# A decoder step on one core: six projection units contraction-outermost in six PSUM banks, modulation weights by 512 columns in buffers of their own

## The chip, the core and the metric

The kernel runs on one core of a Trainium2 chip. The metric is the device time of one execution in microseconds. TensorE (PE) multiplies and transposes into PSUM (8 banks of 512 float32 per partition), ScalarE (ACT), VectorE (DVE) and GpSimd (POOL) do the elementwise work, SyncE's queue (SP) issues nearly all loads from HBM, strictly in the order written. Each engine runs its own program; they meet in semaphores.

## What is computed

One layer for 256 prompt tokens and 8 x 4 sample tokens (288 columns, TOK). Cut to what matters:

```python
mod = (silu(c) @ w_ada + b_ada).reshape(B, 6, 1, D)     # w_ada: 1024 x 6144
sh1, sc1, g1, sh2, sc2, g2 = [mod[:, i] for i in range(6)]
h = x * (1 + sc1) + sh1
qa, ka, va, qb, kb, vb, ga, gb = split(h @ w_in)        # w_in: 1024 x 5120
# rotary on q and k; dilated attention (A) and block attention (B), with caches
merged = sigmoid(ga) * (oa @ w_pa) + sigmoid(gb) * (ob @ w_pb)
x = layer_norm(ALPHA * x + g1 * (merged @ w_o))
h2 = x * (1 + sc2) + sh2
up, gt = split(h2 @ w_up);  f = (silu(gt) * up) @ w_down
x = layer_norm(ALPHA * x + g2 * f)
```

The new keys and values, and shifted caches, are outputs too.

## The kernel before

Activations lie transposed: 8 blocks (KT) of 128 channels by 288 tokens. A projection is done in **units** of 128 output columns (`unit_mm`, L668): for each of 8 contraction blocks three matmuls of 288 columns (`mm3`, L662: high x high, high x low, low x high of a float32 split in two), 24 in one PSUM bank, then an eviction. A unit therefore can't start before its bank is free nor finish before all of h is there. The weights of one unit are a **half**: ScalarE copies it to `w_hi` (L473), VectorE writes the remainder to `w_lo` (L478). There are four places for halves (SPLIT), and ACT and DVE split half nb + 4 right behind the eviction of unit nb.

All weights arrive through one ring, `raw`, of three slots of 1 MB (RAW). `free_slot` (L523) makes SP wait until the piece three before has been used: a piece of w_in, w_up and so on once both halves are split (`lo_ready`), a modulation chunk once its matmuls are done (`ada_used`).

**Modulation** (`ada_mm`, L681): silu(c), 9 rows padded to 32, is the stationary operand; a chunk of 256 columns of w_ada needs eight matmuls, four at a time in the four 32-column strips of the array. ScalarE copies the result to `rowbuf` (`ada_rows`, L1119), TensorE turns it and sums the strips (`ada_turn`, L693, two matmuls), VectorE adds the bias (`ada_add`, L1371). There are 24 chunks: 8 before the projection (shift and scale of h), 12 one by one between the unit pairs, 2 at the output projection and 2 at the second modulation.

**The projection** runs over c = 0 to 11, two units each, in banks 0 and 1; six of the c are queries or keys of which ACT makes a first copy (L1150), DVE a shuffled one (L1428) and POOL and DVE the rotation (the list ROPED); c = 6, 7, 8 and 11 are values. Then eight steps j transpose values and keys to rows (L768), then `keys_turn` (L784) transposes the cached keys of the samples, with scores, gate units and so on behind.

**SP's order** in the projection: w_in pieces and modulation chunks in turn; the masks; from the ninth piece on the cached keys of sample 0 to 3 (`load_kv`, L556, five DMAs each) between them; then the first two pieces of gate weights (GATE0, GATE0 + 1, L606) behind the last piece of the projection; only then a wait for the transposes. The first two gate halves are split in the last pair but one's order, as nb + 4 says.

Of the kernel before, what the change touches and what calls it, by code (L numbers as in the profile page):

```python
# [7 lines left out]
F32 = mybir.dt.float32  # L8
# [177 lines left out]
MIX_N = 12  # L186
# [91 lines left out]
def build(nc, x_prompt, x_sample, cache_a, cache_rows, cache_b, page_table, c_prompt, c_sample, w_ada, b_ada, w_in,  # L278
# [24 lines left out]
    kvin, _ = sb("kvin", [128, 2, 6, 256])  # L303
# [7 lines left out]
    rowbuf, _ = sb("rowbuf", [128, 3, 256])  # L311
# [3 lines left out]
    rows, _ = sb("rows", [64, 128])  # L315
# [42 lines left out]
    st6, _ = sb("st6", [128, 3, 4, 6])  # L358
# [19 lines left out]
    c_zero, c_ready, ada_used, first_in = sem("c_zero"), sem("c_ready"), sem("ada_used"), sem("first_in")  # L378
# [53 lines left out]

    def raw_half(n_static_slot, hh, by_rows):

        if by_rows:
            return raw[:, n_static_slot, 1024 * hh:1024 * hh + 1024]
        return raw8(n_static_slot)[:, :, 128 * hh:128 * hh + 128]
# [22 lines left out]
    def part(t, slot, by_rows):  # L460
        if by_rows:
            return t[:, slot, :]
        return t[:, slot, :].rearrange("p (k n) -> p k n", k=8)

    def split_hi(act, nb, slot4, rslot, hh, need, by_rows=False):

        if isinstance(nb, int) and nb == 0:
            act.wait_ge(first_in, 16)
        else:
            act.wait_ge(raw_in[rslot], need)  # L470
# [32 lines left out]

    PAB_BANK = (0, 1, 6, 3)
# [14 lines left out]
    def _(sp):  # L519
# [3 lines left out]
        def free_slot(n):  # L523

            m = n - RAW
            if m >= 0 and ada_chunk(m) is not None:
                sp.wait_ge(ada_used, N_ADA_BEFORE[m] + 1)
# [6 lines left out]

        def load_ada(n):
            a = ada_chunk(n)
            load(n, n % RAW, w_ada_v[:, :, 256 * a:256 * a + 256], raw8(n % RAW))

        for n in range(MIX0):
            load_ada(n)  # L540
            if n == 0:
                sp.dma_start(rows[0:48, :], b_ada.rearrange("a (j p) -> (a j) p", p=128)).then_inc(rows_in, 16)
                sp.dma_start(rows[48:56, :], ln1_g.rearrange("a (j p) -> (a j) p", p=128)).then_inc(rows_in, 16)
                sp.dma_start(rows[56:64, :], ln1_b.rearrange("a (j p) -> (a j) p", p=128)).then_inc(rows_in, 16)
            if n == 2:
                sp.dma_start(x_tok[:, 0:2, :], x_prompt.rearrange("a (t p) d -> p (a t) d", p=128)).then_inc(x_in, 16)
                sp.dma_start(x_tok[0:SAMPLE, 2, :], x_sample.rearrange("b t d -> (b t) d")).then_inc(x_in, 16)
# [38 lines left out]

        for n in range(MIX0, GATE0):
            c = (n - MIX0) // 2
            if n == MIX0:
                free_slot(n)  # L590
                sp.dma_start(raw8(n % RAW)[:, :, 0:128], w_in_v[:, :, 0:128]).then_inc(first_in, 16)
                sp.dma_start(raw8(n % RAW)[:, :, 128:256], w_in_v[:, :, 128:256]).then_inc(raw_in[n % RAW], 16)
                sp.dma_start(cst[:, C_COS:C_MS], const[:, C_COS:C_MS]).then_inc(tables_in, 16)
                sp.dma_start(pages[:], page_table.rearrange("b n -> (b n)").unsqueeze(0)).then_inc(pages_in, 16)
            elif ada_chunk(n) is None:
                load(n, n % RAW, w_in_v[:, :, 256 * c:256 * c + 256], raw8(n % RAW))
            else:
                load_ada(n)
            if n == MIX0 + 9:
                sp.dma_start(cst[:, C_MS:C_END], const[:, C_MS:C_END]).then_inc(masks_in, 16)  # L600
                sp.wait_ge(pages_in, 16)
            if MIX0 + 9 <= n < MIX0 + 9 + DEC_B:
                look_up_pages(n - MIX0 - 9)
            if n > MIX0 + 9 and n % 2 and (n - MIX0 - 11) // 2 < 4:
                load_kv((n - MIX0 - 11) // 2, 0)
# [72 lines left out]
    def ada_bank(i):  # L678
        return {20: 5, 21: 4, 22: 7, 23: 2}.get(i, 5 + i % 3)

    def ada_mm(pe, n):  # L681

        i, slot, bank = N_ADA_BEFORE[n], n % RAW, ada_bank(N_ADA_BEFORE[n])
        pe.wait_ge(raw_in[slot], raw_need(n, slot))
        if i >= 3:
            pe.wait_ge(ada_mod, i - 2)
        for k in range(KT):
            q = 32 * (k % 4)
            mm = nc.tensor.matmul(psum[q:q + 32, bank, 0:256], c_z[:, k, :], raw8(slot)[:, k, :], start=(k < 4), stop=(k >= 4),  # L689
                                  skip_group_check=True)  # L690
        mm.then_inc(ada_used, 1)

    def ada_turn(pe, i):  # L693

        pe.wait_ge(ada_row, i + 1)
        for hh in range(2):
            mm = nc.tensor.matmul(psum[:, ada_bank(i), 256 + 9 * hh:256 + 9 * hh + 9], rowbuf[:, i % 3, 128 * hh:128 * hh + 128],  # L697
                                  cst[:, C_ADA:C_ADA + 9], start=True, stop=True, skip_group_check=True)
        mm.then_inc(ada_turned, 1)

# [5 lines left out]
    def _(pe):  # L706
# [22 lines left out]
        for i in range(N_ADA0):  # L729
# [1191 lines left out]
```

## Time and profile before

| | us |
|---|---|
| median of 3 runs | 564.42 |
| lowest, highest | 560.51, 568.14 |
| the profiled execution | 561.89 |
| its span | 560.3 |
| PE busy | 516.1 (92%) |
| DVE busy | 290.5 (52%) |
| ACT busy | 223.5 (40%) |
| POOL busy | 92.2 (16%) |

PE's busy time is modelled, since matmuls are pipelined: PE at 92% waits little, but may be at half pace. Where the first matmuls run, the distance between their starts tells the pace. Times of rows are microseconds from the start of the span.

### The profile page before, as it was taken

How to read it: one execution, taken by the hardware profiler on the slowest of the kernel's cores; microseconds unless marked ns; L12 is line 12 of the kernel's file. 1: busy time of each engine (PE TensorE's matmuls, PEld its weight loads, DVE VectorE, ACT ScalarE, POOL GpSimd, SP SyncE). 2: the span in 40 equal slices, each digit the busy share in tenths (PEclk: the TensorE clock that was granted, in tenths of full speed). 3: DMA queues.
4: the chain of work that ended last, by engine and by line, in shares of the span. 5: the costliest groups of instructions: out<-in, count | busy, mean ns of one | idle time of the engine just before them, and what ended most of it. 6: DMA issues, size and time to landing. Idle time of an engine off the chain costs nothing.

```text
span 560.3 us, 10315 instructions
## 1 busy us (share of the span) xinstructions
PE 516.1 (92%) x4051; PEld 473.0 (84%) x4051; DVE 290.5 (52%) x561; ACT 223.5 (40%) x377; POOL 92.2 (16%) x127
## 2 busy tenths in 40 slices
PE   4787999999999989999989979999999999999990
PEld 2546899989978979897789869999999999999980
DVE  0055657556743453353587595546555544435356
ACT  1042424333344454253643645465444344333311
POOL 1000123002770000000055053601111100000005
PEclk9999899999999999998999979999999999999995
DMA  8987699998185982194433474898876745354002
GB/s 280 340 267 231 208 359 348 338 303 293 38 285 173 303 279 77 42 274 142 151 116 114 148 225 132 302 329 289 264 278 216 272 159 182 120 187 171 17 1 84
DMA packets 96719, 116.78 MB, mean 208 GB/s; under 512 B 3596, under 2 KB 87756, under 8 KB 96165
## 3 DMA queue, kind: packets, MB, share of 16 engines
q1 hardware_dynamic: 94788, 102.76, 56.3%
q0 software_dynamic: 1888, 13.44, 6.6%
q8 instruction: 30, 0.49, 0.4%
q14 instruction: 13, 0.10, 0.1%
HBM read 112.90 MB, written 13.57 MB: 226 GB/s over the span
## 4 chain that ended last, share of the span: by engine, by line
PE 77%; DMA 9%; DVE 4%; ACT 3%; SPq 2%; issue 2%; POOL 2%; POOLq 0%; DVEq 0%; ACTq 0%
PE psum L664 21%; PE psum L666 20%; PE psum L665 20%; DMA raw<-in_w_in 6%; PE psum L689 3%; PE psum L784 3%; DMA raw<-in_w_ada 2%; PE psum L900 2%; PE psum L697 2%; PE psum L844 1%; PE psum L886 1%; DVE w_lo L478 1%; PE psum L853 1%; PE psum L798 1%; ACT qkvg L1206 1%
## 5 line engine op out<-in xcount | busy, mean ns | idle before, releaser
L478 DVE TENSOR_TENSOR w_lo<-raw,w_hi 128x1024 fp32r<-128x1024 f32 x118 | 146.7, 1244 | 169.6 <-ACT w_hi L473 169.4
L664 PE MATMUL psum<-act_hi,w_hi 128*128 128x288 f32 x736 | 223.9, 304 | 9.2 <-DVE act_lo L1647 3.5
L665 PE MATMUL psum<-act_lo,w_hi 128*128 128x288 f32 x736 | 219.6, 298 | 0.0
L666 PE MATMUL psum<-act_hi,w_lo 128*128 128x288 f32 x736 | 219.0, 298 | 0.0
L473 ACT ACTIVATE w_hi<-raw 128x1024 fp32r<-128x1024 f32 x118 | 124.1, 1056 | 138.3 <-PE psum L666 90.7
L664 PEld LDWEIGHTS psum<-act_hi,w_hi 128*128 128x128 f32 x736 | 140.5, 191 | 17.9 <-issue 11.0
L666 PEld LDWEIGHTS psum<-act_hi,w_lo 128*128 128x128 f32 x736 | 141.0, 192 | 0.0
L665 PEld LDWEIGHTS psum<-act_lo,w_hi 128*128 128x128 f32 x736 | 140.8, 191 | 0.1
L664 PE MATMUL psum<-f_hi,w_hi 128*128 128x288 f32 x176 | 52.4, 298 | 0.6 <-DVE f_t L1685 0.6
L665 PE MATMUL psum<-f_lo,w_hi 128*128 128x288 f32 x176 | 51.9, 295 | 0.0
L666 PE MATMUL psum<-f_hi,w_lo 128*128 128x288 f32 x176 | 51.8, 294 | 0.0
L1789 POOL TENSOR_TENSOR qkvg<-qkvg,cst 128x288 f32 (+1 forms) x16 | 16.6, 1036 | 121.0 <-ACT qkvg L1150 121.0
L689 PE MATMUL psum<-raw,c_z 128*32 128x256 f32 x384 | 32.4, 468 | 4.4 <-DMA raw<-in_w_ada 4.3
L664 PEld LDWEIGHTS psum<-f_hi,w_hi 128*128 128x128 f32 x176 | 33.0, 187 | 0.9 <-issue 0.8
L666 PEld LDWEIGHTS psum<-f_hi,w_lo 128*128 128x128 f32 x176 | 33.1, 188 | 0.0
L665 PEld LDWEIGHTS psum<-f_lo,w_hi 128*128 128x128 f32 x176 | 33.0, 188 | 0.0
L1823 POOL TENSOR_TENSOR qkvg<-qkvg,gated 128x288 f32<-128x288 f32 x8 | 8.4, 1079 | 120.0 <-DVE gated L1597 120.0
L697 PEld LDWEIGHTS psum<-cst,rowbuf 128*128 128x128 f32 x96 | 16.0, 235 | 11.9 <-ACT rowbuf L1121 6.2
L1874 POOL DMA_DIRECT2D out<-in_cache_kv_a x24 | 11.7, 488 | 77.4 <-PE psum L666 75.8
L689 PEld LDWEIGHTS psum<-raw,c_z 128*32 128x32 f32 x384 | 11.5, 125 | 13.3 <-DMA raw<-in_w_ada 5.4
L1314 ACT ACTIVATE silu_t<-psum 128x288 f32<-128x288 f32 x22 | 9.0, 409 | 33.5 <-PE psum L666 33.5
L697 PE MATMUL psum<-cst,rowbuf 128*128 128x9 f32 x96 | 16.7, 284 | 5.0 <-ACT rowbuf L1121 5.0
(190 smaller groups left out, 556.4 us busy)
## 6 DMA issues: line engine op xcount, KB each, us to landing
raw<-in_w_ada SPq DMA_DIRECT2D x24, 1024.0 KB, 7.1
raw<-in_w_up SPq DMA_DIRECT2D x22, 1024.0 KB, 7.0
raw<-in_w_in SPq DMA_DIRECT2D x19, 1024.0 KB, 7.0
raw<-in_w_down SPq DMA_DIRECT2D x10, 1024.0 KB, 5.0
out<-in_cache_kv_a POOLq DMA_DIRECT2D x16, 504.0 KB, 6.1
raw<-in_w_o SPq DMA_DIRECT2D x4, 1024.0 KB, 4.8
kvin<-in_cache_kv_a SPq DMA_DIRECT2D x8, 256.0 KB, 3.1
kvin<-in_cache_kv_b SPq DMA_DIRECT2D x16, 128.0 KB, 3.4
```

What stands on the lines that cost most here:

```text
L473: nc.scalar.activation(part(w_hi, slot4, by_rows), raw_half(rslot, hh, by_rows), ACT.Copy).then_inc(hi_ready, 1)
L478: nc.vector.tensor_tensor(part(w_lo, slot4, by_rows), raw_half(rslot, hh, by_rows), part(w_hi, slot4, by_rows).bitcast(F32), ALU.subtract) ...
L664: nc.tensor.matmul(out, hi_l, hi_r, start=start, stop=False, skip_group_check=True)
L665: nc.tensor.matmul(out, hi_l, lo_r, start=False, stop=False, skip_group_check=True)
L666: return nc.tensor.matmul(out, lo_l, hi_r, start=False, stop=stop, skip_group_check=True)
L689: mm = nc.tensor.matmul(psum[q:q + 32, bank, 0:256], c_z[:, k, :], raw8(slot)[:, k, :], start=(k < 4), stop=(k >= 4), skip_group_check=True)
L697: mm = nc.tensor.matmul(psum[:, ada_bank(i), 256 + 9 * hh:256 + 9 * hh + 9], rowbuf[:, i % 3, 128 * hh:128 * hh + 128], cst[:, C_ADA:C_ADA ...
L784: mm = nc.tensor.transpose(psum[:, bank, col:col + nr], kv_tiles(b, 0, tile)[0:nr, 0, 128 * hp:128 * hp + 128], cst[0:nr, 0:nr])
L900: mm = nc.tensor.matmul(psum[:, 6, E * i:E * i + E], prbT[:, u % 2, 128 * n:128 * n + 128], tok[:, kb, 1, 256 * g + E * h:256 * g + E * h ...
L1314: nc.scalar.activation(silu_t[:, q, :], psum[:, q, 0:TOK], ACT.Silu).then_inc(silu_ready, 1)
L1789: nc.gpsimd.tensor_tensor(block_at(qkvg, blk), block_at(qkvg, blk), cst[:, C_COS:C_COS + TOK], ALU.mult).then_inc(cos_done, 1)
L1874: pool.dma_start(kv_sample[g][bass.ds(b, 1), 0:BUF[g] - DEC_T, :], cache_rows[g][bass.ds(b, 1), DEC_T:BUF[g], :]).then_inc(moved, 16)
```

## The change

- Modulation weights are read by 512 columns and half of the contraction: a **part** q is 4 contraction blocks x 512 columns, 1 MB as before, four matmuls of 512 columns. Two parts (2i, 2i + 1) add up in a bank; one row copy of 512, one turn of four matmuls and one add follow for both. Parts 0 to 19 go to five buffers `ada_s`, which lie in space that is unused so early: two in `qkvg`'s value and query blocks, one in its gate blocks, where later keys of sample 2 lie, one in `kvin`, one in `tmp`, where later keys of sample 3 lie. Parts 20 to 23 still use the ring.
- Of w_in, blocks 12 to 17 (the values, c = 6 to 8) come first, as four ring pieces of 2 contraction blocks x 768 columns. Their six units run contraction-outermost in banks 0 to 5: step k does all six units' three matmuls of block k. So step 0 needs only h's first block. Splits are of 768 columns, one for each k.
- The other nine c (MIX_C) follow as before, with 12 parts spread over the nine rounds m (MIX_ADA: 2, 1, 1, 2, 1, 1, 2, 1, 1), and six turns, each between a round's two units.
- SP loads in the order shown. Keys of samples 0 and 1 are issued behind part 19; those of sample 2 wait for 19 parts used and those of sample 3 for 20; the gate weights stand behind them.
- Units are counted anew (H_MIX 8, H_GATE 26, was 0 and 24), so slots of halves and of the ring shift.

```diff
+MIX_C = (0, 1, 2, 3, 4, 5, 9, 10, 11)
+FIRST_BLK, FIRST_N = 12, 6
+ADA_ORDER = (0, 2, 1, 3, 4, 5, 6, 7, 8, 9, 10, 11)
+ADA_BANK = (6, 7, 6, 7, 6, 7, 6, 7, 6, 7, 5, 7)
+ADA_BUF = (0, 1, 2, 3, 4, 0, 1, 2, 3, 4, 2, 3, 4, 2, 3, 4, 2, 4, 2, 4)
+MIX_ADA = [range(N_ADA0 + (4 * m + 2) // 3, N_ADA0 + (4 * m + 6) // 3) for m in range(9)]
...
+        def load_start(q):
+            last = [p for p in range(q) if ADA_BUF[p] == ADA_BUF[q]]
+            if last:
+                sp.wait_ge(ada_used, last[-1] + 1)
+            sp.dma_start(ada_s[ADA_BUF[q]][:], ada_part(q)).then_inc(start_in[ADA_BUF[q]], 16)
...
+        load_start(2)
+        load_start(3)
+        load_start(4)
+        load_start(5)
+        load_first(0)
+        load_first(1)
+        load_start(6)
+        load_start(7)
+        load_first(2)
+        load_first(3)
...
+        load_start(8)
+        load_start(9)
+        load_mix(0)
+        load_start(10)
+        load_mix(1)
+        load_mix(2)
+        load_mix(3)
+        load_start(11)
...
+        load_mix(7)
+        load_start(17)
+        load_start(18)
+        load_mix(8)
+        load_start(19)
+        load_kv(0, 0)
+        load_kv(1, 0)
+        sp.wait_ge(ada_used, 19)
+        load_kv(2, 0)
+        sp.wait_ge(ada_used, 20)
+        load_kv(3, 0)
         load_static(GATE0)
         load_static(GATE0 + 1)
...
+    def first_mm(pe, k):
+
+        pe.wait_ge(lo_ready, k + 1)
+        pe.wait_ge(h_lo, k + 1)
+        for q in range(FIRST_N):
+            c = 128 * q
+            mm = mm3(psum[:, q, 0:TOK], w_hi[:, k % SPLIT, c:c + 128], w_lo[:, k % SPLIT, c:c + 128], act_hi[:, k, :], act_lo[:, k, :],
+                     k == 0, k == KT - 1)
...
+        ada_start(pe, 0)
+        ada_start(pe, 1)
+        ada_turn(pe, 0)
+        pe.wait_ge(rows_ready, 1)
+        turn_x()
+        ada_start(pe, 2)
+        ada_start(pe, 3)
+        ada_turn(pe, 1)
+        ada_start(pe, 4)
+        ada_start(pe, 5)
+        first_mm(pe, 0)
+        ada_turn(pe, 2)
+        first_mm(pe, 1)
+        ada_start(pe, 6)
+        ada_start(pe, 7)
+        first_mm(pe, 2)
+        ada_turn(pe, 3)
+        for k in range(3, KT):
+            first_mm(pe, k)
+
+        for m in range(9):
+            for q in MIX_ADA[m]:
+                ada_start(pe, q)
             for hh in range(2):
...
+                nb = H_MIX + 2 * m + hh
+                pe.wait_ge(acc_free[hh], m + 1)
+                unit_mm(pe, nb, nb % SPLIT, hh)
+                if hh == 0 and m in ROWS_AT:
+                    ada_turn(pe, ROWS_AT[m])
```

On ACT the last two rounds of the projection and the first eviction of the transposing steps. Before (L1150 evicts a unit, L473 splits a half, L1121 copies rows, raw_in2 is the ring slot of the first gate weights):

```order
L1121 ACTIVATE rowbuf<-psum 128x256 [waits ada_used]
L1150 ACTIVATE qkvg<-psum 128x288 [waits half_used]
L473 ACTIVATE w_hi<-raw 128x1024 [waits half_used,raw_in2]
L1150 ACTIVATE qkvg<-psum 128x288 [waits half_used]
L473 ACTIVATE w_hi<-raw 128x1024 [waits half_used,raw_in2]
L1121 ACTIVATE rowbuf<-psum 128x256 [waits ada_used]
L1159 ACTIVATE tok<-psum 128x2x128 [waits tok_turned]
```

Of the change, the same place (L1245, L484 and L1203 are the same three operations; raw_in1 is the slot of the first gate weights; the last L1203 copies the rows of parts 18 and 19):

```order
L1245 ACTIVATE qkvg<-psum 128x288 [waits half_used]
L484 ACTIVATE w_hi<-raw 128x1024 [waits half_used,raw_in1]
L1245 ACTIVATE qkvg<-psum 128x288 [waits half_used]
L484 ACTIVATE w_hi<-raw 128x1024 [waits half_used,raw_in1]
L1203 ACTIVATE rowbuf<-psum 128x512 [waits ada_used]
L1252 ACTIVATE tok<-psum 128x2x128 [waits tok_turned]
```

In both the two splits of the gate weights stand around the second eviction of the last round but one and ahead of the last row copy; what differs is when the weights are issued. On SP, before (L533 a ring piece, L559 the first of the five DMAs of a sample's keys), the last six pieces of the projection and the two of the gate:

```order
L565 DMA k_late<-in_cache_kv_b 128x256
L533 DMA raw<-in_w_in 128x8x256 [waits ada_used]
L533 DMA raw<-in_w_ada 128x8x256 [waits lo_ready]
...
L533 DMA raw<-in_w_in 128x8x256 [waits ada_used]
L533 DMA raw<-in_w_in 128x8x256 [waits lo_ready]
L559 DMA k_extra<-in_cache_kv_a 128x256 [waits tok_turned]
```

Of the change (L545 a ring piece, L594 to L600 keys), behind the last modulation part:

```order
L594 DMA k_early<-in_cache_kv_a 128x256 [waits ada_used]
...
L594 DMA k_late<-in_cache_kv_a 128x256 [waits ada_used]
L595 DMA k_late<-in_cache_kv_a 128x2x256
L597 DMA k_late<-in_cache_kv_a 64x1x256
...
L600 DMA k_late<-in_cache_kv_b 128x256
L545 DMA raw<-in_w_in 128x8x256 [waits lo_ready] x2
L594 DMA k_extra<-in_cache_kv_a 128x256 [waits tok_turned]
```

The keys of sample 3 (k_late), which stood before the last modulation chunks, now stand behind the last one's use, with the gate weights (x2) behind them.

## Rows read from the trace of the kernel before

**Rows 1.** Chain of waits, 0 to 200 us: start, length, what.
```profile
10.30 10.03 DMA raw<-in_w_ada
...
50.81 5.22 DMA raw<-in_w_in
...
131.53 0.34 PE psum L697 x4
131.87 1.00 PE psum L689 x16
...
139.45 0.35 PE psum L697 x4
...
153.17 5.42 PE psum L784 x36
```

**Rows 2.** Stretches: length; busy of PE, PEld, DVE, ACT, POOL; granted clock, DMA share, GB/s.
```profile
4.00:28.00 24.00, 16.48 (x113) 10.42 (x116) 1.27 (x7) 1.78 (x5) 0.00 (x0) 1.00 1.08 349
28.00:32.00 4.00, 4.00 (x36) 1.92 (x28) 0.18 (x1) 1.36 (x3) 0.00 (x0) 1.00 0.32 89
58.00:60.00 2.00, 2.00 (x22) 1.42 (x22) 1.97 (x5) 1.01 (x2) 1.03 (x1) 0.83 0.09 28
60.00:147.00 87.00, 86.30 (x724) 80.01 (x723) 52.06 (x112) 28.35 (x44) 18.25 (x37) 0.98 0.88 291
```

**Rows 3.** Timeline of PE, 43 to 64 us: start, length, line, idle before.
```profile
44.03 0.61 PE L664 MATMUL psum<-act_hi,w_hi 128*128 128x288 f32 x1 [3.17 <-DVE w_lo L478]
...
48.76 0.44 PE L665 MATMUL psum<-act_lo,w_hi 128*128 128x288 f32 x1
49.00 0.35 PE L666 MATMUL psum<-act_hi,w_lo 128*128 128x288 f32 x1
49.18 0.30 PE L664 MATMUL psum<-act_hi,w_hi 128*128 128x288 f32 x1
...
57.43 0.61 PE L697 MATMUL psum<-cst,rowbuf 128*128 128x9 f32 x4 [3.29 <-ACT rowbuf L1121]
...
62.70 0.33 PE L665 MATMUL psum<-act_lo,w_hi 128*128 128x288 f32 x1
```

**Rows 4.** Timeline of PE, 8 to 24 us, modulation chunks and a turn.
```profile
12.76 1.03 PE L697 MATMUL psum<-cst,rowbuf 128*128 128x9 f32 x4
...
20.37 1.94 PE L689 MATMUL psum<-raw,c_z 128*32 128x256 f32 x16 [3.61 <-DMA raw<-in_w_ada]
```

**Rows 5.** Timeline of DVE and ACT, 28 to 48 us and 142 to 145.
```profile
29.97 1.08 ACT L1132 ACTIVATE xT<-psum 128x512 f32<-128x512 f32 x2
...
35.23 0.23 DVE L1383 TENSOR_TENSOR qkvg<-xT,mod 128x64 f32<-128x64 f32 x1
...
35.75 0.74 DVE L1387 TENSOR_SCALAR qkvg<-xT,mod 128x256 f32<-128x256 f32 x2
...
39.17 2.29 DVE L1392 TENSOR_TENSOR act_lo<-qkvg,act_hi 128x288 fp32r<-128x288 f32 x6
...
46.17 2.36 DVE L478 TENSOR_TENSOR w_lo<-raw,w_hi 128x1024 fp32r<-128x1024 f32 x2 [0.32 <-ACT w_hi L473]
...
143.29 0.81 DVE L1443 COPY qz<-qkvg 64x32 f32<-64x32 f32 x4
```

**Rows 6.** Timeline of ACT and of SP's queue: a late split, key and gate loads.
```profile
56.05 1.06 ACT L473 ACTIVATE w_hi<-raw 128x1024 fp32r<-128x1024 f32 x1 [5.85 <-DMA raw<-in_w_in]
...
105.41 0.58 SPq L559 DMA_DIRECT2D k_late<-in_cache_kv_a  x1
...
108.56 0.50 SPq L533 DMA_DIRECT2D raw<-in_w_in  x1
...
132.93 2.09 SPq L533 DMA_DIRECT2D raw<-in_w_in  x2
...
151.55 0.34 SPq L559 DMA_DIRECT2D k_extra<-in_cache_kv_a  x1
...
153.15 0.98 SPq L565 DMA_DIRECT2D k_extra<-in_cache_kv_b  x2
```

More of the change, by code:

```diff
@@ L431, in raw8, with raw4 @@
         return raw[:, slot, :].rearrange("p (k n) -> p k n", k=8)
+    def raw4(slot):
+        return raw[:, slot, :].rearrange("p (k n) -> p k n", k=4)
     def raw_half(n_static_slot, hh, by_rows):
+        if by_rows == "first":
+            return raw[:, n_static_slot, FIRST_COLS * hh:FIRST_COLS * hh + FIRST_COLS]
         if by_rows:
@@ L460, in part @@
     def part(t, slot, by_rows):
+        if by_rows == "first":
+            return t[:, slot, 0:FIRST_COLS]
         if by_rows:
@@ L465, in split_hi @@
     def split_hi(act, nb, slot4, rslot, hh, need, by_rows=False):
[L467 to L470, printed above, removed]
+        act.wait_ge(raw_in[rslot], need)
         if not isinstance(nb, int) or nb >= SPLIT:
@@ L484, in halves @@
         for n in range(first, last):
-            by_rows = PAB0 <= n < WO0 or n >= DOWN0
+            by_rows = "first" if n < MIX0 else PAB0 <= n < WO0 or n >= DOWN0
             for hh in range(n_halves(n)):
@@ L502, in lo_static @@
             split_lo(dve, nb, s, r, hh, by)
+    ROWS_AT = {m: q // 2 for m, qs in enumerate(MIX_ADA) for q in qs if q % 2}
     PAB_BANK = (0, 1, 6, 3)
@@ L533, in load, with ada_part @@
             sp.dma_start(dst, src).then_inc(raw_in[slot], 16)
+        def ada_part(q):
+            j, a = ADA_ORDER[q // 2], q % 2
+            return w_ada_v[:, 4 * a:4 * a + 4, 512 * j:512 * j + 512]
         def load_ada(n):
[L536 to L547, printed above, removed]
+            load(n, n % RAW, ada_part(ada_chunk(n)), raw4(n % RAW))
@@ L585, in load_static, with load_mix @@
                 load(n, n % RAW, w_up_v[:, :, col:col + 256], raw8(n % RAW))
[L587 to L605, printed above, removed]
+        def load_mix(m):
+            n, c = MIX0 + m, MIX_C[m]
+            load(n, n % RAW, w_in_v[:, :, 256 * c:256 * c + 256], raw8(n % RAW))
+        load_start(8)
[6 more added lines that the diff above has]
+        load_start(11)
+        sp.dma_start(cst[:, C_MS:C_END], const[:, C_MS:C_END]).then_inc(masks_in, 16)
+        sp.wait_ge(pages_in, 16)
+        look_up_pages(0)
+        look_up_pages(1)
+        load_mix(4)
+        load_start(12)
+        look_up_pages(2)
+        look_up_pages(3)
+        load_mix(5)
+        load_start(13)
+        load_start(14)
+        look_up_pages(4)
+        look_up_pages(5)
+        load_mix(6)
+        load_start(15)
+        load_start(16)
+        look_up_pages(6)
+        look_up_pages(7)
+        load_mix(7)
[9 more added lines that the diff above has]
+        load_kv(3, 0)
         load_static(GATE0)
@@ new lines, in _ @@
+        for j in range(2):
+            dve.wait_ge(turned_x, j + 3)
+            V.tensor_copy(xT[:, 4 * j:4 * j + 4, 128:256],
+                          psum[:, 3 + j, :].rearrange("p (k c) -> p k c", c=128)).then_inc(x_ready_dve, 1)
+        dve.wait_ge(turned_x, 5)
+        V.tensor_copy(xT[:, :, PROMPT:TOK], psum[:, 0, 0:256].rearrange("p (k c) -> p k c", c=SAMPLE)).then_inc(x_ready_dve, 1)
+        dve.wait_ge(x_ready_act, 2)
+        dve.wait_ge(x_ready_dve, 3)
+        ada_add(1)
+        modulate_pair(0)
@@ L1420, in _ @@
+        lo_static(dve, 5)
         rest_of(qkvg, 6, h_hi, h_lo)
         rest_of(qkvg, 7, h_hi, h_lo)
-        for nb in range(H_MIX + 1, H_MIX + AHEAD):
+        for nb in range(6, 11):
             lo_static(dve, nb)
+        for q in (1, 3, 5):
+            if q < 5:
+                dve.wait_ge(first_done, q + 1)
+            else:
+                dve.wait_ge(half_used, KT)
+            V.tensor_copy(qkvg[:, FIRST_BLK + q, :], psum[:, q, 0:TOK]).then_inc(acc_free[1] if q == 1 else v_free, 1)
@@ L1578, in _ @@
         oT_rest(1)
-        ada_add(20)
         def merged_rest(m):
```

269 lines of the change are left out of this document (137 added, 132 removed).

## Prediction, made before the changed kernel ran

> **What bounds the kernel now.** I read the chain of waits of the first 200 us, the stretches beside it, and then TensorE's own instructions. The chain [rows 1] shows two stages. Up to 59 us it hangs on loads and on what follows them: 10.03 us for a piece of w_ada, 5.22 us for a piece of w_in issued at 50.81. From there it is TensorE almost alone: between the turns at 131.53 and 139.45 lie 7.92 us, which are 0.34 for the turn, 1.00 for one modulation chunk and 6.58 for two projection units, 24 matmuls each. In 60 to 147 TensorE is busy 86.3 of 87 us [rows 2]. The units end one such round behind 139.45, at 147.4, eight transposing steps follow, and key turning (L784) begins at 153.17. What the change can win must come from before 59 us, where six units' work can be put under the loads; after that only the sum of TensorE's work counts, and any new wait adds to it.
>
> The loads of the start are not at their limit throughout: 349 GB/s in 4 to 28, but 89 in 28 to 32 and 28 in 58 to 60, because the three-slot ring waits for its readers [rows 2]. At 349 GB/s a piece of 1.05 MB takes 3.0 us.
>
> **TensorE's pace.** The first unit starts at 44.03, one matmul of 288 columns each 0.24 us, which is 1.2 GHz; from 49.18 on it is the pace of 6.58 us for 48 matmuls, 0.137 each with its gaps, 2.4 GHz. The ring then starves it 3.29 us (to 57.43), and up to 62.70 the pace is 0.24 again [rows 3]; the granted clock, 1.00 in most rows, is 0.83 in 58 to 60 [rows 2], so I go by the starts of matmuls. The modulation matmuls before 40 us all ran at the slow pace: 1.94 us a chunk, 1.03 a turn of two matmuls [rows 4].
>
> **Step 1: the start.** First load, second load, x, and the next two modulation parts carry the same bytes as the three chunks, x and the fourth chunk did, so the fourth part lands at 20.4, as the fourth chunk did [rows 4]. Behind it, in issue order at 3.0 us for 1.05 MB and 2.3 for the 0.79 MB pieces of w_in: parts 5 and 6 at 23.4 and 26.4, w_in 0 and 1 at 28.7 and 30.9, parts 7 and 8 at 33.9 and 36.9, w_in 2 and 3 at 39.2 and 41.5. Buffers of their own let them follow without a gap. TensorE: parts 3 and 4 end about 23.7, their turn (now four matmuls, 2.0 us slow, after a row copy of 1.08/2 = 0.54) at 26.4, parts 5 and 6 at 30.3. VectorE's two modulations take twice 0.23, then 0.74 for two blocks, and gaps, 1.3 us a pair; splitting 768 columns takes three quarters of 1.18 on VectorE, 0.9, and as much on ScalarE; a rest (act_lo) is 2.29/6 = 0.4 [rows 5]. The first of the eight steps of the six-bank stage then starts at about 31, when w_in 0 is split: 18 matmuls, 4.3 us slow or 2.4 fast. In order: step 0 to 35.3; turn to 37.3; step 1, mostly fast, to 40; parts 7 and 8 (2.0) to 42; step 2 to 44.4; turn (0.7) to 45.1; step 3 to 47.5. Step 4 needs the second half of h: add, two modulation pairs, a split and a rest, 0.2 + 2.6 + 0.9 + 0.4 behind the turn, so 49.2, a wait of 1.7. Four more steps: **58.9**. By then the old kernel had done two units and ten chunks; this one has done six units and eight.
>
> **Step 2: the remaining 18 units.** Nine rounds of 6.58 [rows 1], twelve parts of 1.00, six turns of twice 0.34: 59.2 + 12.0 + 4.1 = 75.3, so they would end at 134.2 against 147.4, a gain of **13.2**. A part of 4 matmuls on 512 columns streams as many columns as 8 on 256. No row has that form; nearest is the chunk, 1.00 fast and 1.94 slow. I take 1.00; without its gaps 0.8 is possible (12 x 0.2 = 2.4 less), and if 512 columns in four strips overlap worse, 1.94 is the far end (11 more). VectorE and ScalarE keep the work per round that they had and have slack: of 87 us VectorE is busy 52 and ScalarE 28 [rows 2].
>
> **Step 3: the wait that the change brings.** Here the listing of the order decides. SP's queue is strictly in order. The fourth set of keys (k_late) now lies where part 19's buffer was, and is issued only after all 20 parts are used; the first gate weights stand behind it. Part 19 is used at the head of the last round. But these gate halves are split two rounds ahead in ScalarE's and VectorE's order, in the last round but one, in front of the eviction of its second unit and of the last row copy. In the old kernel the gate weights were issued at 132.93, 14.5 us before the units ended [rows 6]. Now: part 19 used at T. The five key loads hold SP 3.1 us (105.41 to 108.56 [rows 6]). The gate load lands 5.2 us after issue with nothing ahead (50.81 to ScalarE's start at 56.05 [rows 1, 6]). Then ScalarE: split 1.06, eviction 0.4, split 1.06, row copy 0.55: T + 11.4. TensorE has in that time only one unit, 3.3; it then waits in the turn of the last rows for **8.1 us**. Behind that turn stand the last unit and all transposes, and VectorE, waiting for the same halves, is no earlier. Bounds: the key loads took 2.6 at least (151.55 to 154.13 [rows 6]), and a load in a full queue 8 (a chunk of 3.0 ahead of it): the wait lies between 7.6 and 11. The clock pays too: after 3.29 us idle the pace was slow for 3.6 us, at the first unit for 5 [rows 3]. So the turn costs 2.0 instead of 0.7, and the last unit has 15 to 20 matmuls at 0.24 instead of 0.134, 1.6 to 2.1: **3.1** together, 0 if the clock held.
>
> **Step 4: the tail.** The four query copies (0.81 [rows 5]) now fall in the last round, ahead of the first key copy: **0.7** later. From there on every wait hangs on what TensorE has done and moves with it; the last two modulation chunks have half the row copies, under half a microsecond, which I leave out. The ring's slots are numbered anew but hold as many pieces.
>
> **Sum.** 13.2 - 8.1 - 3.1 - 0.7 = 1.3 us earlier at L784. The profiled execution takes 561.9 (span 560.3, and what lies around it stays), so 560.6. It lies 2.5 below the median of 564.4; on the median's scale the sum is 563.1. I forecast **561.5**, between the two. (2%, about what a measurement of this kernel can tell, is 11.3 us.)
>
> **Rivals.**
> The gate wait is hidden: slower key turning or the sequence of semaphores lets the last unit run first. For it: all the weights but these are long there. Against: T + 11.4 has no cover but one unit, and even the shortest key loads leave 7.6. It gives 561.9 - (13.2 - 0.7) = 549.4. A cheaper cousin, parts at 0.8, no slow clock and the shortest wait, gives 560.6 - 2.4 - 3.1 - 0.5 = 554.6.
>
> The slower side: the contraction-outermost stage never gets the fast clock. Its steps are 2.4 us bursts between waits and modulation matmuls, and the modulation matmuls alone ran at the slow pace for 20 us though TensorE was busy [rows 4]. Seven more steps at 0.24 cost 18 x 0.106 x 7 = 13.4, less the 1.7 of the wait, plus 2.6 for two parts and a turn: 14.3 more, 574.9 on the profile's scale, 577 on the median's. Each slow step costs 1.9, so one undoes the 1.3 of the sum, and with seven the change is slower by 2%. Against: the longest pause in my order is 1.7, and 1.35 us of turn and chunk between units never slowed it in 60 to 147.
> The Trainium skill, TensorE: Matmul & The Clock Gate, section HAM oscillation, speaks for this rival: a kernel that walks the contraction and waits for a load between its steps falls back to 1.2 GHz each time, and it advises finishing the contraction of one output before waiting. By that rule the time would be the rival's 574.9; the trace's pause of 3.29 us agrees with the rule, but no row has so short a pause as the ones here.
>
> A second late load: the weights of the last round are issued behind part 18, whose buffer frees only in round 6 (109.8), and land about 118 (a second load lands 3 after the first). ScalarE then evicts round 6's second unit late, and its bank is free about 120.8, 1.4 us before TensorE wants it. If loads are 2 or 3 us slower, TensorE waits 1 to 2 more there and the key loads move along: 562 to 565.
>
> **Numbers.** Forecast as summed 0.67 (its own range 556 to 567); gate wait hidden or mostly paid back 0.13; slow clock in the six-bank stage 0.06; second late load 0.10; something else in the ring 0.04. The range 551 to 568 leaves out part of the hidden wait and the slow clock. Faster by over 2% (below 553.1) 0.14, slower 0.06, between 0.80.
>
> **What would show it.** Right: the first matmul of six banks near 31, the stage over near 59 with a 1 to 2 us gap before step 4; rounds of 7.6 or 8.3 or 9.3; a DMA of w_in issued near 130 in the chain, TensorE idle about 8 us before the last turn, slow pace behind it; L784's first turn near 151 to 152. Wrong: no idle stretch near 130, a six-bank stage over after 65 with steps of 4.3, or parts that take other than 1.0.

## The result, and the profile after

| | before | after |
|---|---|---|
| median of 20 runs each | 563.17 | 566.10 |
| lowest, highest | 559.09, 568.14 | 563.32, 569.53 |
| ratio after to before, with its 95% interval | | 1.006 (1.0036 to 1.0084) |
| span of the profiled execution | 560.3 | 564.4 |
| PE busy | 516.1 | 510.9 |
| DVE, ACT, POOL busy | 290.5, 223.5, 92.2 | 294.4, 222.9, 89.1 |

The change makes the kernel 0.6% slower, where about 0.5% faster was forecast (561.5 against the 564.42 known then). TensorE is busy 5.2 us less and the span is 4.1 us longer, so about 9 us of waits have come in. The line numbers of after that matter: L721 to L723 are `mm3`, L742 the matmuls of a part, L756 the turn, L484 and L489 the splits on ScalarE and VectorE, L1203 the row copy, L1549 the query copies, L852 and L853 the transposes of values and keys, L868 key turning, L1911 GpSimd's scaling of x, L545 a ring load.

The chain of waits of after, 120 to 156 us (start, length, what), from the last modulation part to key turning:

```profile
122.83 1.04 PE psum L742 x8
123.89 0.34 SPq L594
...
126.49 5.88 DMA raw<-in_w_in
...
133.74 0.94 ACT w_hi L484
134.69 0.50 ACT rowbuf L1203
135.22 1.88 PE psum L756 x8
...
142.47 0.46 DVE qkvg L1561
143.03 4.66 DVE qz L1549
...
149.05 0.66 PE psum L852 x2
...
154.17 1.95 PE psum L868 x13
```

Before, these 30 us were nearly all TensorE ([rows 1]: a turn, a chunk, units). Now they hold two stalls: the gate load that was forecast, and behind it 4.66 us in one query copy of VectorE, which was not. Key turning starts at 154.17, 1.0 later than in [rows 1].

The stretches of after (columns as in [rows 2]):

```profile
4.00:28.00 24.00, 16.30 (x97) 8.03 (x97) 4.92 (x14) 4.29 (x9) 0.00 (x0) 0.86 1.03 388
28.00:32.00 4.00, 3.32 (x15) 3.35 (x16) 3.61 (x10) 2.79 (x6) 0.00 (x0) 0.61 1.05 410
...
130.00:140.00 10.00, 4.78 (x21) 4.78 (x22) 4.49 (x8) 2.79 (x4) 3.87 (x17) 0.57 0.48 158
140.00:155.00 15.00, 10.16 (x68) 9.00 (x68) 10.54 (x22) 4.25 (x16) 7.49 (x11) 0.83 0.08 24
```

The start answers to [rows 2]: 388 GB/s where 349 were moved, 410 where 89 were. From 130 to 155 TensorE is busy 14.9 of 25 us, at a granted clock of 0.57 and 0.83.

The timeline of TensorE in after, the six-bank stage and the start of the nine rounds behind it (idle before in brackets):

```profile
23.87 1.92 PE L742 MATMUL psum<-ada_s,c_z 128*32 128x512 f32 x16
28.68 0.39 PE L721 MATMUL psum<-act_hi,w_hi 128*128 128x288 f32 x1 [2.88 <-DVE act_lo L1483]
...
32.67 0.95 PE L756 MATMUL psum<-cst,rowbuf 128*128 128x9 f32 x8
...
45.41 0.37 PE L721 MATMUL psum<-act_hi,w_hi 128*128 128x288 f32 x1 [1.58 <-DVE act_lo L1483]
55.12 1.92 PE L742 MATMUL psum<-ada_s,c_z 128*32 128x512 f32 x16
```

The stage starts at 28.68 and is over at 55.12, 3.8 us before the forecast.

### The profile page after: what moved, and what is told of

Read it like the earlier page. It is cut to its first block, busy times and chain, and to the rows that moved or that the text cites. A ratio compares the mean times of both kernels' runs of the same rounds, so it can differ in the third digit from the quotient of the medians.

```text
span 564.4 us, 9903 instructions
## 1 busy us (share of the span) xinstructions
PE 510.9 (91%) x3859; PEld 464.0 (82%) x3859; DVE 294.4 (52%) x548; ACT 222.9 (39%) x370; POOL 89.1 (16%) x127
## 4 chain that ended last, share of the span: by engine, by line
PE 81%; DMA 6%; DVE 6%; issue 2%; ACT 2%; SPq 2%; POOL 1%; POOLq 0%; DVEq 0%; ACTq 0%
PE psum L721 22%; PE psum L723 21%; PE psum L722 21%; DMA raw<-in_w_in 5%; PE psum L742 3%; PE psum L868 3%; PE psum L984 2%; PE psum L756 1%; PE psum L928 1%; DMA ada_s<-in_w_ada 1%; PE psum L970 1%; PE psum L937 1%; PE psum L882 1%; DVE qz L1549 1%; ACT w_hi L484 1%
## 5 line engine op out<-in xcount | busy, mean ns | idle before, releaser
L721 PE MATMUL psum<-act_hi,w_hi 128*128 128x288 f32 x736 | 224.6, 305 | 8.9 <-DVE act_lo L1483 4.5
L489 DVE TENSOR_TENSOR w_lo<-raw,w_hi 128x1024 fp32r<-128x1024 f32 (+1 forms) x120 | 147.1, 1228 | 163.0 <-ACT w_hi L484 162.8
L723 PE MATMUL psum<-act_hi,w_lo 128*128 128x288 f32 x736 | 219.5, 298 | 0.0
L484 ACT ACTIVATE w_hi<-raw 128x1024 fp32r<-128x1024 f32 (+1 forms) x120 | 124.6, 1041 | 128.0 <-PE psum L723 96.1
L721 PEld LDWEIGHTS psum<-act_hi,w_hi 128*128 128x128 f32 x736 | 141.0, 192 | 22.1 <-issue 13.9
L723 PEld LDWEIGHTS psum<-act_hi,w_lo 128*128 128x128 f32 x736 | 141.2, 192 | 0.0
L721 PE MATMUL psum<-f_hi,w_hi 128*128 128x288 f32 x176 | 52.4, 298 | 0.6 <-DVE f_t L1787 0.6
L723 PE MATMUL psum<-f_hi,w_lo 128*128 128x288 f32 x176 | 51.8, 294 | 0.0
L721 PEld LDWEIGHTS psum<-f_hi,w_hi 128*128 128x128 f32 x176 | 33.0, 187 | 0.9 <-issue 0.8
L723 PEld LDWEIGHTS psum<-f_hi,w_lo 128*128 128x128 f32 x176 | 33.2, 188 | 0.0
L1891 POOL TENSOR_TENSOR qkvg<-qkvg,cst 128x288 f32 (+1 forms) x16 | 14.5, 906 | 117.4 <-ACT qkvg L1245 117.4
L756 PEld LDWEIGHTS psum<-cst,rowbuf 128*128 128x128 f32 x96 | 12.6, 203 | 14.4 <-ACT rowbuf L1203 14.4
L742 PE MATMUL psum<-ada_s,c_z 128*32 128x512 f32 x160 | 23.1, 683 | 0.6 <-DMA ada_s<-in_w_ada 0.6
L756 PE MATMUL psum<-cst,rowbuf 128*128 128x9 f32 x96 | 12.7, 260 | 10.2 <-ACT rowbuf L1203 10.2
L1245 ACT ACTIVATE qkvg<-psum 128x288 f32<-128x288 f32 x16 | 6.5, 408 | 36.1 <-PE psum L723 36.1
```

The costliest lines, as they stand in the source:

```text
L484: nc.scalar.activation(part(w_hi, slot4, by_rows), raw_half(rslot, hh, by_rows), ACT.Copy).then_inc(hi_ready, 1)
L489: nc.vector.tensor_tensor(part(w_lo, slot4, by_rows), raw_half(rslot, hh, by_rows), part(w_hi, slot4, by_rows).bitcast(F32), ALU.subtract) ...
L721: nc.tensor.matmul(out, hi_l, hi_r, start=start, stop=False, skip_group_check=True)
L723: return nc.tensor.matmul(out, lo_l, hi_r, start=False, stop=stop, skip_group_check=True)
L742: mm = nc.tensor.matmul(psum[32 * kk:32 * kk + 32, ADA_BANK[i], :], c_z[:, 4 * a + kk, :], src[:, kk, :], start=(a == 0), stop=(a == 1), s ...
L756: mm = nc.tensor.matmul(psum[:, ADA_BANK[i], 9 * hh:9 * hh + 9], rowbuf[:, i % 2, 128 * hh:128 * hh + 128], cst[:, C_ADA:C_ADA + 9], start ...
```

## The experiments

Nine kernels ran; all times are in us. The first four shared one chip and its runs of the kernel before (median 563.63), the next four another (562.86), the last one a third series (562.19). Where two of my kernels are compared, it is by the spans and rows of their profiles, and by the ratio to before where that is said.

**Queries a round earlier.** Why did a copy of 64 x 32 elements take 4.7 us? The order on VectorE puts the query copies behind the last unit's eviction; GpSimd, which waits only for the last rotation, is by then in its long scaling of x (6.04). This kernel makes the copies one round (m) earlier.

```diff
-            if m == 8:
+            if m == 7:
                 queries_by_row(3)
```

> The changed kernel, with the last four query copies one round earlier on VectorE (m = 7, their inputs are long there). In the changed kernel they take 5.31 us together, where the kernel before had 0.81, beside a 6.04 us operation of GpSimd (the scaling of x). Theory A: they are held by GpSimd's operation running at the same time; moved to where GpSimd is between its rotation and its key copies they take about 1 us, key turning starts 4 to 5 us earlier than 154.17 (149 to 150), the time falls by 4 to 5 us to about 561.5 and the wait of 8.0 us before the last turn stays. Theory B: the copies are slow because of what they read (a wait or a bank of their inputs), then they stay near 5 us wherever they stand and the time stays at 566.

Measured: median 556.3 (555.25 to 559.65), ratio 0.988 (0.982 to 0.995), span 554.0. The copies and GpSimd's scaling in this run (two rows of the timelines of DVE and POOL):

```profile
138.69 0.81 DVE L1549 COPY qz<-qkvg 64x32 f32<-64x32 f32 x4
...
142.81 6.04 POOL L1911 TENSOR_SCALAR xT<-xT 128x2304 f32<-128x2304 f32 x1
```

and in after:

```profile
141.62 6.04 POOL L1911 TENSOR_SCALAR xT<-xT 128x2304 f32<-128x2304 f32 x1
...
142.95 5.31 DVE L1549 COPY qz<-qkvg 64x32 f32<-64x32 f32 x4
```

Ahead of the scaling four copies take 0.81; begun 1.3 us into it they take 5.31, and the first alone ends at 147.71, 0.05 behind the scaling's end at 147.66. Key turning starts at 148.62, 5.5 earlier than in after, while the wait for the gate weights stays (8.96). So the two stalls are separate. The gain in the span, 10.4 (9.8 by the medians), is more than the 5.5 at key turning and more than the 4 to 5 expected: further on, TensorE's pause ahead of the prompt's transposes shrinks from 3.54 to 1.81 and no slow matmuls follow it (3.2 together), and the second group of matmuls on the sample values takes 3.00 instead of 4.61 (4.52 before, so that part is not an effect of the copies alone).

**Gate weights first.** This takes the forecast wait away by issuing the two loads ahead of the keys that wait for parts 18 and 19.

```diff
         load_kv(1, 0)
+        load_static(GATE0)
+        load_static(GATE0 + 1)
         sp.wait_ge(ada_used, 19)
         load_kv(2, 0)
         sp.wait_ge(ada_used, 20)
         load_kv(3, 0)
-        load_static(GATE0)
-        load_static(GATE0 + 1)
```

> The changed kernel, with the first two pieces of gate weights issued on SP ahead of the keys of samples 2 and 3, so that they wait for nothing that the last round does. Theory A: TensorE's wait of 8.0 us ahead of the last turn goes, and with it the slow pace of the turn and of the last unit (1.1 and 2.0 us): 11 us less up to the end of the units (about 131 instead of 142.3). GpSimd's scaling of x follows the last rotation, so it begins near 131 and still meets the query copies: those stay near 5 us. Time about 555. Rival: another load takes the place (the key loads of sample 3 or the weights of the last round), the wait only shrinks to 3 to 5 us and the time is 560 to 563.

Measured: median 555.02 (549.56 to 559.1), ratio 0.987 (0.979 to 0.994), span 548.0. TensorE ahead of the last turn, and the chain's gate load:

```profile
128.96 1.06 PE L756 MATMUL psum<-cst,rowbuf 128*128 128x9 f32 x8 [1.29 <-ACT rowbuf L1203]
```

```profile
117.02 9.08 DMA raw<-in_w_in
```

The wait falls from 8.02 to 1.29, the slow pace behind it is gone (the turn takes 1.06, not 1.88), and key turning starts at 139.18, 15.0 earlier. Of these, 6.7 are the wait, about 3 the clock, and the rest is the copies: they took 0.77, where I had expected them to stay near 5. They ran at 133.82, GpSimd's scaling began at 135.38. So the meeting of the two came from the late gate weights. They delay both engines, but not equally. GpSimd's last rotation waits for an eviction that stands behind the gate split in ScalarE's order; in after:

```profile
133.82 1.54 POOL L1891 TENSOR_TENSOR qkvg<-qkvg,cst 128x288 f32<-128x288 f32 x1 [12.78 <-ACT qkvg L1245]
```

In this kernel that rotation starts at 127.55, after 6.12 idle. The scaling thus comes 6.2 later in after than here (141.62 for 135.38), and the copies 9.1 later (142.95 for 133.82). The 2.9 between the two is what the slow clock adds to the turn (0.8) and to the last unit (about 2.0), which stand ahead of the copies alone. It turns a lead of 1.6 over the scaling into a lag of 1.3.

The profiled execution took 549.56, for the 549.4 of my rival "the gate wait is hidden"; but it is the fastest of the four, and the median is 555.02.

**Both.**

> Both edits together. If the two waits are apart, the savings add: 11 and 4.5 to 5 us from 566, about 550, key turning near 138 to 139. If GpSimd's scaling then holds the key copies of the transposing steps instead (before the change it ran beside them at no visible cost), only one of the two is saved: 555.

Measured: median 549.29 (547.15 to 550.51), ratio 0.974 (0.967 to 0.980), span 547.8; wait before the last turn 1.24, copies 0.81, key turning at 138.50. It is faster than the kernel before and than the changed one. By its profile it equals the one with the gate weights first alone (547.8 and 548.0), so with the gate weights early the move of the queries adds next to nothing in the rows; that the medians differ by 5.7 is not explained by them. The kernel with only the gate weights first ranged over 9.5 us, and its profile shows its fastest execution; what the slower ones did is not on record.

**GpSimd's scaling moved behind its stores,** with the query copies where the change has them: the rival cause for the long copy was something in the copies' own place (their source, just evicted).

```diff
         pool.wait_ge(new_keys, 24)
-        nc.gpsimd.tensor_scalar(xT[:], xT[:], ALPHA, None, ALU.mult).then_inc(x_scaled, 1)
...
                 pool.dma_start(dst, src).then_inc(done, 16)
+        nc.gpsimd.tensor_scalar(xT[:], xT[:], ALPHA, None, ALU.mult).then_inc(x_scaled, 1)
```

> The changed kernel, with GpSimd's scaling of x behind its stores of new keys and values instead of ahead of them; the query copies stay in the last round. Theory A (GpSimd's operation holds VectorE's copies): the copies fall from 5.31 to about 0.8 us though they stand where they stood; key turning starts 4 to 5 us earlier and the time is about 561.5, the same as with the copies moved. Theory B (something else in that place holds them): they stay near 5 us and the time stays near 566.

Measured: median 559.75 (557.29 to 563.18), ratio 0.9945 (0.991 to 0.998), span 558.9. The timeline of VectorE at the copies, and of GpSimd:

```profile
143.33 0.73 DVE L1549 COPY qz<-qkvg 64x32 f32<-64x32 f32 x4
```

```profile
139.65 2.60 POOL L1909 COPY q_rows<-qkvg 64x32 f32<-64x32 f32 x16
...
160.37 6.06 POOL L1922 TENSOR_SCALAR xT<-xT 128x2304 f32<-128x2304 f32 x1
```

Same copies, same place, no scaling beside them: 0.73. Key turning at 148.66. That shows the cause. Where the scaling went, it met another operation of VectorE that reads and writes SBUF, the split of a gate half. The same split here and in the kernel with the earlier queries:

```profile
162.11 4.96 DVE L489 TENSOR_TENSOR w_lo<-raw,w_hi 128x1024 fp32r<-128x1024 f32 x1 [0.98 <-ACT w_hi L484]
```

```profile
162.07 1.23 DVE L489 TENSOR_TENSOR w_lo<-raw,w_hi 128x1024 fp32r<-128x1024 f32 x1 [0.98 <-ACT w_hi L484]
```

It ended 0.64 behind the scaling. That set the chain back by about 0.7. Further on the fifth gate load took 8.64 instead of 7.40, the pause ahead of the prompt's transposes was 3.25 instead of 1.81, and 17 slow matmuls followed; whether that comes from the split is not shown. The span is 4.9 longer than with the earlier queries, the median 3.5 longer, and the intervals of the two ratios overlap.

**Rows of 1 KB, and their control.** The six-bank stage came 3.8 us early, and the loads were faster than in [rows 2]. Two things differ there for the modulation weights: rows of 2 KB instead of 1 KB, and buffers of their own. In the first of these kernels the first eight parts are read by two loads of 256 columns each (1 KB rows), in the second by two loads of two contraction blocks each (2 KB rows).

```diff
+            if q < 8:
+                for i in range(2):
+                    sp.dma_start(ada_s[ADA_BUF[q]][:, :, 256 * i:256 * i + 256], ada_part(q)[:, :, 256 * i:256 * i + 256]).then_inc(start_in[ADA_BUF[q]], 16)
+                return
             sp.dma_start(ada_s[ADA_BUF[q]][:], ada_part(q)).then_inc(start_in[ADA_BUF[q]], 16)
...
-        ada_mm(pe, q, ada_s[ADA_BUF[q]], start_in[ADA_BUF[q]], 16 * ADA_BUF[:q + 1].count(ADA_BUF[q]))
+        ada_mm(pe, q, ada_s[ADA_BUF[q]], start_in[ADA_BUF[q]],
+               sum(32 if p < 8 else 16 for p in range(q + 1) if ADA_BUF[p] == ADA_BUF[q]))
```

> The changed kernel, but each of the first eight modulation parts is read by two loads of 256 columns: rows of 1 KB in HBM and in the buffer instead of 2 KB, the same bytes and buffers, eight more issues. The six-bank stage was over at 55.1 us, 3.8 before the forecast, and the loads ran at 388 GB/s in 4 to 28 instead of 349. Theory A, the longer rows: the stretch falls back to near 350 GB/s, the first matmul of six banks moves from 28.7 to 30 to 31, the stage ends at 58 to 59, and the time is 2 to 4 us longer than the changed kernel's 566. Theory B, the buffers of their own (loads in flight without a gap): 380 to 390 GB/s stay and the stage ends within 0.7 of 55.1.

> The control of the run with 1 KB rows: the same first eight parts are read by two loads each too, but of two contraction blocks by 512 columns, so with rows of 2 KB. Theory A and B alike: 380 to 390 GB/s in 4 to 28, the six-bank stage over within 0.7 of 55.1, the time within 2 of the changed kernel's. If it too falls back to 350 GB/s, it is the number of loads or their issues and not the rows.

Measured: 566.85 (564.03 to 568.97) with a span of 562.9, and 568.97 (565.98 to 570.46) with a span of 566.9. The stretch 4 to 28 of the first and of the second:

```profile
4.00:28.00 24.00, 18.89 (x93) 10.35 (x97) 4.24 (x14) 3.62 (x7) 0.00 (x0) 1.00 1.06 375
```

```profile
4.00:28.00 24.00, 16.33 (x97) 9.05 (x97) 4.52 (x14) 3.90 (x8) 0.00 (x0) 1.00 1.03 387
```

Halving the rows costs 12 to 13 of the 39 GB/s that the change had won; the other 26 stay. What is left to explain them are the buffers of their own and the pieces of w_in, whose rows are now 3 KB (768 columns); neither was tried by itself. The first matmul of six banks came at 29.59, 0.9 later than in after, but the stage was over at 55.3, not at 58 to 59: theory A falls.

The control kept its 387 GB/s and yet was over only at 57.1, where within 0.7 of 55.1 was expected, and its median is 2.9 above that of after, where within 2 was expected (ratio to before 1.011, 1.005 to 1.018, which overlaps with that of after). What differs is TensorE's pace. In the kernel with 1 KB rows TensorE had no pause ahead of the stage and came to the fast pace during step 0:

```profile
31.20 0.39 PE L725 MATMUL psum<-act_hi,w_hi 128*128 128x288 f32 x1
31.42 0.30 PE L726 MATMUL psum<-act_lo,w_hi 128*128 128x288 f32 x1
31.55 0.29 PE L727 MATMUL psum<-act_hi,w_lo 128*128 128x288 f32 x1
```

In the control it paused 3.20, ran nine matmuls at the fast pace, and then starts stayed 0.24 apart up to 37.1; in after it paused 2.88 and they were 0.24 apart up to 32.2. But this is not an effect of the rows: the kernels with whole parts, which have the same instructions up to here, differ as well. In one below it paused 1.58 and step 0 ran at the fast pace, the stage over at 54.2; in the last one it did not pause, its modulation matmuls were slow, and the stage was over at 55.8. With 2 KB rows and 386 to 391 GB/s the end lies between 54.2 and 57.1, and the stage itself takes 25.0 (54.2) to 28.0 (57.1). Its last four steps take the same 9.7 in all of them, so the difference lies in TensorE's pace in and before the first steps, and it changes from one profiled execution to the next.

Both kernels also repeat the meeting of copies and scaling. Begun 1.9 and 0.6 us into it, the copies took 4.71 and 6.05, and ended 0.6 behind it both times, as in after.

**The third gate piece early,** on top of the kernel with both mends. Behind key turning the chain runs over a load of w_in with TensorE idle ahead of the prompt's transposes (3.54 in after, 2.50 before).

```diff
         load_kv(3, 0)
+        load_static(GATE0 + 2)
...
-        load_static(GATE0 + 2)
         for b in range(2):
```

> The version with both mends (queries copied a round earlier, the first two gate pieces issued ahead of the keys of samples 2 and 3), and the third piece of gate weights issued behind the keys of sample 3 instead of behind all sample keys. There the chain ran over this load (issued 174.44, 7.67 to landing) and TensorE was idle 3.58 us before the prompt's transposes, with 9 slow matmuls behind. Theory: the load decides that pause; it goes to under 1.5 us, the slow pace behind it goes too, and the span falls by 3 to 5 us, from 547.8 to 543 to 545. Rival: the mask and split work of VectorE before the transposes decides it; the pause stays at 2.5 or more, and whether slow matmuls follow goes by that length; the span falls by under 1.5.

Measured: 547.21 (544.09 to 548.9), ratio 0.973 (0.967 to 0.980), span 544.4. TensorE ahead of the prompt's transposes, in the kernel with both mends and in this one:

```profile
186.70 1.36 PE L970 MATMUL psum<-cst,prb 128*128 128x128 f32 x6 [3.57 <-ACT prb L1287]
```

```profile
185.30 0.88 PE L970 MATMUL psum<-cst,prb 128*128 128x128 f32 x6 [1.98 <-ACT prb L1287]
```

The pause fell by 1.6, to 1.98 and not to under 1.5 as expected, and the slow pace went. But I had named the wrong load: the chain still ran over one of w_in, issued at 173.56 and 7.16 in coming. It is the fifth gate piece, behind a wait for sample scores and a set of values.

**The first two gate pieces ahead of all keys,** on top of that.

```diff
+        load_static(GATE0)
+        load_static(GATE0 + 1)
         load_kv(0, 0)
         load_kv(1, 0)
-        load_static(GATE0)
-        load_static(GATE0 + 1)
```

> The kernel with the early third gate piece, and the first two gate pieces issued ahead of the keys of samples 0 and 1 too. There SP spent 108.9 to 116.9 on ten issues of keys before the first gate load, which took 9.0 us to land, and TensorE waited 1.24 us before the last turn. Theory: issued near 109 it lands by 118, two us before its split's turn, the wait goes from 1.24 to under 0.3, and the time falls by about 1. Rival: the loads ahead of it are then the bound (the last projection piece and the last modulation part, which land in the same queue), or the sample keys come late at key turning near 138 and cost there what is won: within 0.5 of the kernel beside it.

Measured: 545.96 (545.37 to 546.6), ratio 0.971 (0.966 to 0.976), span 544.8. No row of TensorE before the last turn has an idle time any more:

```profile
126.16 0.96 PE L756 MATMUL psum<-cst,rowbuf 128*128 128x9 f32 x8
```

Key turning begins 2.9 earlier than in the kernel beside it (135.6 against 138.5, of which 1.4 come from the six-bank stage), but the pause ahead of the prompt's transposes is 3.62 again, with slow pace, and takes it back:

```profile
184.03 1.31 PE L970 MATMUL psum<-cst,prb 128*128 128x128 f32 x6 [3.62 <-ACT prb L1287]
```

The load of the fifth piece, issued at 171.03, took 8.42 here and 7.16 there. An earlier TensorE waits the longer for a late load.

**All gate pieces among the sample keys,** the test of that load, on top of that. The fourth and the fifth piece move.

```diff
         load_kv(4, 0)
+        load_static(GATE0 + 3)
         for b in range(5, DEC_B):
...
+        load_static(GATE0 + 4)
         for b in range(2):
             sp.wait_ge(kt_turned, 14 + b)
             load_kv(b, 1)
-        load_static(GATE0 + 3)
         sp.wait_ge(scored_s, 4)
         load_kv(2, 1)
-        load_static(GATE0 + 4)
```

> The kernel with the first three gate pieces early, and the fourth and fifth piece of gate weights issued among the sample keys as well (behind those of sample 4 and of sample 7) instead of behind the first value loads. The run with only the third piece early showed that I had named the wrong load: the one in the chain at 173.56 is the fifth, issued behind a wait for the sample scores and a set of values, and landing at 180.7 just before its split; the idle time before the prompt's transposes was 1.98 there and 3.62 with slow pace in the run beside it. Theory: the fifth piece decides this pause. With its slot free at 149.5 and issued near 151 it is in place when ScalarE comes to it, the pause falls below 1, the slow pace behind it goes, and the span falls from 544.8 to 540 to 541.5. Rival: VectorE's masks and ScalarE's exponentials decide; the pause stays above 2 and the span within 1 of 544.

Measured: median 545.1 (542.74 to 549.4), ratio 0.975 (0.966 to 0.983), span 541.2. The same row of TensorE:

```profile
182.24 0.82 PE L970 MATMUL psum<-cst,prb 128*128 128x128 f32 x6
```

No pause and no slow pace: gate loads decided it. The chain names the fifth piece; since the fourth moved too, the run does not tell them apart. The profile is 3.6 shorter than that of the kernel beside it; the ratios (0.971 and 0.975) overlap, so the runs don't show that gain, and I count the kernel with both mends and the last three as equal by time, 2.5 to 3% below before.

## Why the prediction was right or wrong

**What bounds the kernel:** right. Behind the six-bank stage the rounds took 67.7 us up to the last one (forecast 67.0), a part 1.04, and before the gate wait TensorE was busy all of 60 to 120.

**Step 1, the start:** right in its mechanism, 3.8 too late (58.9 forecast, 55.1 measured). The pause before step 4 was 1.58 for 1.7. Two terms were mis-sized. The loads: 3.0 us for 1 MB came from a stretch with 1 KB rows and the ring of three slots; at 388 to 410 GB/s it is 2.6 to 2.7, and the first step started at 28.7 instead of 31. And the clock: I kept parts 5 and 6 and the turn behind step 0 at the slow pace (3.9 and 2.0); they took 1.92 and 0.95.

**Step 2:** right (a part 1.04 for 1.00, the rounds as above).

**Step 3, the gate wait:** right, and the best-supported part.

```profile
132.39 1.06 ACT L484 ACTIVATE w_hi<-raw 128x1024 fp32r<-128x1024 f32 x1 [12.31 <-DMA raw<-in_w_in]
```

```profile
135.22 1.88 PE L756 MATMUL psum<-cst,rowbuf 128*128 128x9 f32 x8 [8.02 <-ACT rowbuf L1203]
```

8.1 was forecast and 8.02 measured, which two small misses helped: the key issues held SP for 2.6 instead of 3.1, and the gate load took 5.9 instead of 5.2; the turn behind it took 1.88 (2.0), and matmuls of the last unit started 0.24 apart up to 141.4. The second kernel took both away and won 15.0 at key turning. The last unit ended at 142.3, where my steps give 145.4: that is step 1's 3.8, less 0.7 in the rounds. With step 4 as forecast, key turning would have begun at 148.8, 4.4 earlier than before; the first experiment, where it began at 148.62, was 1.2% faster than before.

**Step 4, the tail, is the step that failed.** The copies, priced at 0.7, took 5.31, and behind them the first four groups of transposes ran at half pace (0.64 a group for 0.33, 1.2 together). From the last unit's end to key turning lie 11.9 us, not 6.5, and key turning began 1.0 later than before, where the sum had 1.3 earlier. I priced the copies by a row of their own engine, and didn't ask what GpSimd does at that moment. Before, its scaling of x ran from 147.39 to 153.43, behind the copies at 143.29 [rows 5]. The change puts the copies behind the last unit, and my own step 3 then delays them more than it delays GpSimd: the gate wait holds both, the slow clock behind it (the 3.1 of the sum) only the copies. So the two orders slid over each other; the second experiment has the numbers.

That the time came out only 4.6 above the forecast is in part luck: up to the last unit the kernel was 3.1 earlier than forecast, which hides that much of the 5.4 lost in the tail and of the 3.1 lost behind it.

The Trainium skill, SBUF — State Buffer, section Who interferes with whom, says that a VectorE instruction that uses both port pairs (a copy within SBUF can) and a GpSimd instruction exclude each other for a whole instruction. The first copy's end 0.05 behind the scaling's, and 0.73 for all four without it, agree. VectorE's copies from PSUM beside the same scaling stayed at 0.42 to 0.46 in before and in the first experiment.

**"From there on every wait moves with TensorE"** failed too. From key turning (+1.0) to the end (+4.1) another 3.1 came in: the fifth gate load was issued 1.64 later and took 7.79 instead of 7.37, so that TensorE paused 3.54 instead of 2.50 ahead of the prompt's transposes, and behind the longer pause twelve matmuls started 0.24 apart, which cost 1.5. The chain of after:

```profile
189.97 7.79 DMA raw<-in_w_in
...
202.34 0.98 PE psum L970 x6
203.32 0.24 PE psum L721
203.56 0.24 PE psum L722
203.80 0.24 PE psum L723
```

and of before at the same place:

```profile
188.33 7.37 DMA raw<-in_w_in
...
200.28 0.87 PE psum L886 x6
201.16 0.14 PE psum L664
```

The last experiment shows that this pause hangs on the gate loads. The remaining half microsecond I leave open.

**The rivals.** The hidden gate wait needed another order on SP's queue; with that the profiled execution took 549.56 for my 549.4 and the median 555.02. The closeness of the first is not the mechanism's doing alone: the start was 3.8 better than forecast, and about as much was lost further on. The slow clock in the six-bank stage did not come: the Trainium skill's HAM oscillation (TensorE: Matmul & The Clock Gate) speaks of a fall to 1.2 GHz behind each load wait between steps, and as I applied it that would have come here. Its example has waits of about 3 to 5 us; the one wait between steps here is 1.58. Behind it the last four steps took 9.7 in every run, 72 matmuls 0.134 apart. What the clock did cost, up to 3 us between the fastest and the slowest stage, lay in the first steps. The second late load did not come: the round before the last had no pause.

## What to carry to other kernels

When a change makes an engine wait, follow every other engine and ask how much later each gets: where one is delayed less than its neighbour there is a new overlap, and a short copy may meet a long operation of GpSimd that it has never met before. Moving that operation elsewhere only helps if nothing of the kind stands there. In an in-order load queue, put a load that something on the critical path needs as far ahead as its buffer allows, before any load that itself waits for a release; here moving two issues was worth some 11 us by the medians. And a forecast pause should be priced with the pace behind it, in every place where it grows, not only in the first.

## What the runs showed of the hardware

- A VectorE copy of 64 x 32 float32 within SBUF, 0.17 to 0.2 us alone, took 4.75 beside a GpSimd operation of 6.04 that had begun 1.3 earlier, and ended 0.05 behind it. A VectorE subtraction of 128 x 1024 with both inputs in SBUF, 1.23 alone, took 4.96 beside the same operation, begun 1.7 into it, and ended 0.64 behind it. VectorE copies from PSUM beside it kept their 0.42.
- In stretches in which loads of 1 MB with 2 KB rows and free buffers prevail, this one core moved 386 to 391 GB/s (4 to 28 us); with 1 KB rows 375; with 1 KB rows and a ring of three slots 349. In 28 to 32, where w_in's pieces with 3 KB rows take part, it was 407 to 410, and 385 in the kernel with 1 KB rows.
- Ahead of the prompt's transposes, pauses of 1.81, 1.98, 2.50, 2.52 and 2.70 us left TensorE at its fast pace, and those of 3.25, 3.50, 3.54, 3.57 and 3.62 were followed by 9 to 17 matmuls at half pace. Ahead of the six-bank stage one of 1.58 cost nothing, and seven of 2.59 to 3.23 were followed by 10 to 20 matmuls at half pace, in four of them only after three to nine fast ones.
- At the fast pace four matmuls of 512 columns in four strips take 1.0 us, as eight of 256 did.
